# Opening of a two-layer streaming encoder on one core: cached latents on the weights' queue, ScalarE's transfers behind its table load

## The reference

```python
def mla_expand(c_kv, k_rope, w_kvup, qk_k_norm):
    kv = (c_kv @ w_kvup).reshape(B, K, MLA_HEADS, MLA_NOPE_DIM + MLA_V_DIM)
    k_nope, v = kv[..., :MLA_NOPE_DIM], kv[..., MLA_NOPE_DIM:]
    kr = jnp.broadcast_to(k_rope[:, :, None, :], (B, K, MLA_HEADS, MLA_ROPE_DIM))
    k = rmsnorm(jnp.concatenate([k_nope, kr], axis=-1), qk_k_norm)
    return k, v
...
lat_all = jnp.concatenate([past[0], c_kv], axis=1)     # 512 cached latents, then the new ones
kr_all = jnp.concatenate([past[1], k_rope], axis=1)
km, vm = mla_expand(lat_all, kr_all, lp['mla_w_kvup'], lp['mla_qk_k_norm'])
```

## Time and profile before

| | us |
|---|---|
| median of 3 runs | 1043.76 (1043.03 to 1043.83) |
| the profiled execution | 1046.98 |
| span of its instructions | 1045.2 |
| TensorE busy | 1038.1 (99%) |
| VectorE busy | 643.9 (62%) |
| ScalarE busy | 506.6 (48%) |
| GpSimd busy | 314.5 (30%) |

### The profile page before, as it was taken

How to read it: one execution, slowest core, us unless ns; L and a number is a source line. 1 busy time by engine, 2 the same in 40 slices (tenths; PEclk the granted TensorE clock), 3 DMA queues, 4 the chain that set the end, 5 groups by cost and what they waited for, 6 DMA issues and landing times.

```text
span 1045.2 us, 20057 instructions
## 1 busy us (share of the span) xinstructions
PE 1038.1 (99%) x7572; PEld 1003.7 (96%) x7572; DVE 643.9 (62%) x1093; ACT 506.6 (48%) x936; POOL 314.5 (30%) x277
## 2 busy tenths in 40 slices
PE   8999999999999999999999999999999999999998
PEld 6899999999999999999988999999999999999998
DVE  6889764445766666543567996554557565565443
ACT  6567755444554444434354585554445444433341
POOL 2365566531221111100132755656312211111000
PEclk9999999999999999999999999999999999999999
DMA  6465533334535444454513544334344354444541
GB/s 223 114 166 139 186 103 121 92 131 142 161 121 166 156 145 156 142 179 146 176 46 117 167 147 139 94 117 122 122 152 152 122 179 141 155 146 145 158 148 64
DMA packets 49146, 146.27 MB, mean 140 GB/s; under 512 B 8792, under 2 KB 14904, under 8 KB 49080
## 3 DMA queue, kind: packets, MB, share of 16 engines
q1 hardware_dynamic: 42464, 142.86, 43.8%
q10 hardware_dynamic: 6616, 2.50, 1.0%
HBM read 142.11 MB, written 3.22 MB: 139 GB/s over the span
## 4 chain that ended last, share of the span: by engine, by line
PE 98%; DVE 1%; issue 1%; ACT 0%; POOL 0%; ACTq 0%; POOLq 0%
PE psum L585 29%; PE psum L586 29%; PE psum L587 29%; PE psum L786 1%; PE psum L825 1%; PE psum L808 1%; PE psum L816 1%; PE psum L858 1%; PE psum L1047 0%; PE psum L913 0%; PE psum L948 0%; PE psum L687 0%; PE psum L850 0%; PE psum L729 0%; PE psum L722 0%
## 5 line engine op out<-in xcount | busy, mean ns | idle before, releaser
L585 PE MATMUL psum<-AH,WH 128*128 128x320 f32 x1328 | 414.3, 312 | 0.2
L587 PE MATMUL psum<-AH,WL 128*128 128x320 f32 x1328 | 410.3, 309 | 0.0
L586 PE MATMUL psum<-AL,WH 128*128 128x320 f32 x1328 | 410.2, 309 | 0.0
L585 PEld LDWEIGHTS psum<-AH,WH 128*128 128x128 f32 x1328 | 249.2, 188 | 7.4 <-issue 5.5
L586 PEld LDWEIGHTS psum<-AL,WH 128*128 128x128 f32 x1328 | 249.3, 188 | 0.2
L587 PEld LDWEIGHTS psum<-AH,WL 128*128 128x128 f32 x1328 | 249.3, 188 | 0.0
L1130 ACT CAST WH<-raw 128x1024 fp32r<-128x1024 f32 x166 | 172.7, 1045 | 123.2 <-PE psum L587 122.4
L1603 DVE TENSOR_TENSOR WL<-raw,WH 128x1024 fp32r<-128x1024 f32 x103 | 128.9, 1252 | 113.4 <-ACT WH L1130 113.1
L2094 POOL TENSOR_TENSOR WL<-raw,WH 128x1024 fp32r<-128x1024 f32 x60 | 147.7, 2478 | 97.7 <-ACT WH L1130 94.8
L1802 DVE TENSOR_TENSOR WL<-raw,WH 128x1024 fp32r<-128x1024 f32 x88 | 107.5, 1222 | 49.6 <-ACT WH L1313 48.3
L2099 POOL TENSOR_TENSOR fab<-fa,fb 128x320 f32<-128x320 f32 x44 | 38.7, 879 | 264.7 <-DVE fb L1807 264.7
(11 more groups left out here) (296 smaller groups left out, 1580.4 us busy)
## 6 DMA issues: line engine op xcount, KB each, us to landing
raw<-w_all SPq DMA_DIRECT2D x264, 512.0 KB, 3.5
y_out<-X SPq DMA_DIRECT2D x8, 160.0 KB, 2.7
X<-x_in SPq DMA_DIRECT2D x2, 320.0 KB, 5.2
X<-x_in SPq DMA_DIRECT2D x1, 640.0 KB, 7.1
lat_out<-ckv ACTq DMA_DIRECT2D x2, 320.0 KB, 2.9
scratch<-brel SPq DMA_DIRECT2D x8, 63.8 KB, 4.2
bias<-scratch SPq DMA_DIRECT2D x8, 48.0 KB, 3.9
ckv<-lat_in ACTq DMA_DIRECT2D x1, 384.0 KB, 4.5
```

The source lines that it names most:

```text
L585: mm(out, WH[:, slot, c0:c0 + cols], high, start=first, stop=False)
L586: mm(out, WH[:, slot, c0:c0 + cols], low, start=False, stop=False)
L587: return mm(out, WL[:, slot, c0:c0 + cols], high, start=False, stop=last)
```

## The change

The first latents are now issued by SP, ahead of the value weights, and the second latents by ScalarE. On ScalarE the wait for the zeros and the square root (with the table load that stands ahead of it) come first; then the rotary rows are issued and then the second latents. The zero products stay as they are (four rounds).

```diff
     @block.sync
     def _(sp):
         lat = lat_in[0:1].rearrange("a p c n -> (a p) c n")
+        sp.dma_start(ckv[:, :, T:T + 128], lat[:, :, 0:128]).then_inc(s.cache_lat[0], 16)
         sp.dma_start(raw[:, U_KVV, :], w_all[stored(U_KVV)]).then_inc(raw_ready[U_KVV], 16)
         sp.dma_start(raw[:, U_KVK, :], w_all[stored(U_KVK)]).then_inc(raw_ready[U_KVK], 16)
-        sp.dma_start(ckv[:, :, T + 128:T + 256], lat[:, :, 128:256]).then_inc(s.cache_lat[1], 16)
         sp.dma_start(cst[:, K_ID:K_ID + 128], cst_in[:, K_ID:K_ID + 128]).then_inc(s.id_in, 16)
...
-        act.dma_start(ckv[:, :, T:T + 128], lat_in[0:1].rearrange("a p c n -> (a p) c n")[:, :, 0:128]) \
-            .then_inc(s.cache_lat[0], 16)
-        rope_cached(0)
         act.wait_ge(s.warm_zero, 1)
         A(small[:, 31:32], ssum[:, 0:1], ACT.Sqrt)
+        rope_cached(0)
+        act.dma_start(ckv[:, :, T + 128:T + 256], lat_in[0:1].rearrange("a p c n -> (a p) c n")[:, :, 128:256]) \
+            .then_inc(s.cache_lat[1], 16)
         act.wait_ge(raw_ready[U_KVV], 16)
```

## The result

The changed kernel is slower: median 1046.42 us (1044.94 to 1047.0, 14 runs) against 1043.8 us (1042.67 to 1044.21, 14 runs) before, a ratio of 1.0023 (95% interval 1.0015 to 1.0030). I had forecast 1041.0. The profiled execution took 1046.56 us, so it is a usual one of its kernel. The profiled execution of before, at 1046.98, is not: none of the 14 runs came above 1044.21. That turns out to matter most.

What follows compares the result with a forecast made beforehand. TensorE, busy nearly throughout, was taken as the bound, its opening held by the first latents. About 1.2 us (clock) plus 1.5 (hole) gave 2.74 us off the 1043.76 median: 1041.0 us, range 1040.0 to 1043.3.

Steps and rivals of the forecast that it cites:

- The start of that square sets everything later: ScalarE's square of the first key block, at 12.24 us; starting it earlier moves the rest of the program as it stands.
- The opening has no reason to differ by that: Profiled execution stood 3.2 us above the median; the opening's gain of 2.74 us was still taken from the median.
- my own forecast of 9.5: Start of the square of the first keys, forecast at 9.5 us instead of 12.24, 2.74 us earlier.
- my threshold: 0.2% (2.1 us), about what a measurement of this kernel can tell from no change.
- Value weights about 5.0: Opening, SP's queue: value weights land about 5.0 us instead of 4.4, the delay covered by the zero products until 5.91.
- Table load first ... issue ends at 3.9: ScalarE's opening: load and root end at 2.75 us, then the rope rows' issue (1.12 us) ends at 3.9.
- the weighing of load and drain: ScalarE's table load: 1.49 us with root, or ending at 4.12 with a 1.38 us drain; hidden-cost rival 1042.0, chance 0.06.
- my 8.3: Landing of the second latents on ScalarE's queue, issued at 3.9 us; at 8.3 nothing is held.
- the rival "slower": Second latents starve on ScalarE's queue; landing at 12.1 loses 0.8 us, 1044.6; chance 0.07, 0.05 by over 0.2%.
- Key weights 7.35: Opening, SP's queue: key weights land at 7.35 us, unchanged, and become the gate.
- The clock: the rival that I gave 0.07: Clock falls again between 9.45 and 12.86; second block's products at 0.43 us, 1.5 us won, 1042.2; chance 0.07.
- 2.4 GHz from about 6 us on: TensorE's granted clock 1.00 from about 6 us, products 0.23 us apart; about 1.2 us of the gain is the clock.

Runs made afterwards that it cites:

- e2: Kernel before with the two latents' queues swapped, but ScalarE's transfers still issued ahead of the table load; median 1046.41 us, ratio 1.0022.
- e8: The changed kernel, unedited, for a second profile; one time, 1046.18 us.
- e1: The kernel before, unedited, for a second profile; median 1043.09 us, profiled 1042.77, ratio 1.000.
- e9: The kernel before with five rounds of zero products instead of four; median 1044.7 us, ratio 1.0001.
- e10: The changed kernel with ScalarE's two opening transfers moved to SP, plus five rounds of zero products; median 1044.29 us, ratio 1.0000.
- e7: The changed kernel with five rounds of zero products instead of four; median 1045.21 us, ratio 1.0006 to the kernel before.
- e5: The changed kernel with ScalarE's two transfers (rotary rows, second latents) issued on SP behind the key weights; median 1044.29 us, ratio 1.0002 to the kernel before.
- e3: Kernel before, queues unchanged, with only ScalarE's wait for zeros, root and table load ahead of its two transfers; median 1044.88 us, ratio 1.0020.
- e6: The changed kernel with first and second latents in one 256 KB transfer, first on SP; median 1046.36 us, ratio 1.0015 to the kernel before.
- e4: The changed kernel with value weights issued ahead of the first latents on SP; median 1044.96 us, ratio 1.0010 to the kernel before.

## Why the prediction was wrong, step by step

**"The start of that square sets everything later": right.** Time of the execution minus start of the square, over all profiles: before 1034.7, after 1034.8, e2 to e8 1034.7 to 1034.9 throughout; e1, e9 and e10 1034.0 to 1034.1. The last three are 0.7 shorter for a reason below. Nothing was lost behind that square. (SP's later issues did start up to 0.5 us later, against the prediction: the third latents at 5.33 instead of 4.84.)

| profile | value weights landed | first value product | square | its time |
|---|---|---|---|---|
| before | 4.4 | 7.96 | 12.24 | 1046.98 |
| e1, before again | 4.3 | 5.62 | 8.71 | 1042.77 |
| after | 6.0 | 6.82 | 11.72 | 1046.56 |
| e8, after again | 5.9 | 6.67 | 11.39 | 1046.18 |
| e7, after with five rounds | 6.4 | 7.15 | 10.32 | 1045.05 |

**"The opening has no reason to differ by that": the step that failed.** I saw the profiled execution stand 3.2 us above the median and still took a gain worked out in its opening off the median. e1 shows where the 3.2 us lay: in that opening. The 6.3 us landing of the earlier trace rows was that execution's; in e1 and in e9 the same transfer took 4.0, and in e1 the hole and the half-rate products that I meant to remove were not there to remove. Against the 8.71 of e1, even my own forecast of 9.5 is a loss of 0.8. Between executions the landing moved by 2.3 us, more than my threshold. How often before shows the late case is not settled: times above 1046.4 came in 0 of the 14 runs of the result and in 0, 4 and 3 of 33, 29 and 21 runs of before in the later sets. Four of these seven (1046.82 to 1047.26) have a mean granted clock of 0.998, as the profiled execution has with its stretch at 0.50; all other runs of these sets have 1.000. No trace of the seven is on record, so their landings are not known.

**"Value weights about 5.0": mis-sized by 1.0.** I charged the later issue and gave them the 3.6 us of a transfer that goes first. They took 4.5 (e8 4.4, e2 4.3, e7 4.9), landed at 6.0, and so the zero products, which ended at 5.91, did not cover them. Of the 1.65 us by which they are later than before (4.4 to 6.0), 0.75 is the issue behind the first latents, 0.3 what standing second costs without ScalarE's transfers (e5: 3.93 for 3.6), and 0.6 the transfers on ScalarE's queue (4.54 against 3.93). Each is a difference of single executions; by e2, e7, e8 and e10 the last lies between 0.3 and 0.9. The windows from 1.5 to 4.0 and from 3.0 to 4.0 us show the bytes (last two columns: share of the DMA engines, GB/s). First the changed kernel, then e1:

```profile
1.50:4.00 2.50, 2.50 (x5) 1.62 (x6) 0.87 (x5) 0.73 (x2) 1.09 (x2) 1.00 0.50 124
...
3.00:4.00 1.00, 1.00 (x3) 0.68 (x2) 0.59 (x2) 0.00 (x0) 0.00 (x0) 1.00 0.60 145
```

```profile
1.50:4.00 2.50, 2.50 (x5) 1.62 (x6) 0.27 (x3) 1.36 (x2) 1.09 (x2) 1.00 0.86 239
...
3.00:4.00 1.00, 1.00 (x3) 0.67 (x2) 0.00 (x0) 0.99 (x2) 0.00 (x0) 1.00 0.95 360
```

In these 2.5 us the changed kernel moved 310 KB (at 124 GB/s), e1 598 KB. The Trainium skill (DMA: Bandwidth & Descriptors, Issuing engines are not separate DMA queues) has transfers of different engines share the same 16 DMA engines; e5 against the change agrees: with ScalarE's transfers beside them the value weights took 4.54 us, without 3.93. But sharing is not all: between 3 and 4 us the engines are busy 0.60 of the time, so they stand partly idle just when the value weights should run. Without ScalarE's transfers (e5) the same microsecond shows 0.71 and 205 GB/s, still far from e1; with them, but issued from 0.75 on (e2), 0.82 and 252, so it does not go by their presence alone. Nor did ScalarE's transfers hold the value weights where these went first: before, e1 and e3 had them beside and took 3.5 to 3.6. What the DMA engines wait for no run here shows; SP's issue of the value weights itself is longer there, 0.58 us for the 0.40 it takes when it goes first.

**"Table load first ... issue ends at 3.9": wrong.** The queue issues while the load runs (1.25 against 0.75 to 2.03). The 1.38 us drain that the Trainium skill (ScalarE: Activation LUTs, What ACT_TABLE_LOAD costs) adds to a load for every switch to a different set is not seen behind this load: the root starts at 2.04, 0.01 us after the load's end. So the weighing of load and drain was idle. The second latents landed at 8.0, near my 8.3, but by luck: issued at 2.48 and 5.5 us on the way. They held nothing; the kernel is slower, but not by the mechanism of the rival "slower", their late landing.

**"Key weights 7.35": right** (7.45, e8 7.4), but no longer the only gate.

**The clock: the rival that I gave 0.07.** I counted on 2.4 GHz from about 6 us on. The products of both profiles of the changed kernel ran at 0.43 spacing to 10.8 and to about 10.2, after TensorE stood idle 0.91 and 0.77 us. I had priced such a stretch in the second block, not from the first product on. It costs 1.4 to 1.8 us: from the first product to the square it is 4.9 and 4.7 us here, 3.1 to 3.3 in e1, e2, e3, e5 and e7. The times bear this out: with a fifth round (e7) the slow group is gone and the median falls by 1.2.

Among holes this short, the length does not decide: after 0.73 us (e2), 1.00 (e3) and 1.19 (e7) the products ran at the full rate. The profiles differ in when the clock rose. In e1, e6, e7 and e9 it rose during the zero products (eight in 3.88 and 3.99 us, ten in 4.70 and 4.73); in before, e2, e3, e4 and e5 the eight kept to 4.61 to 4.64 us, and the clock had risen by the first value product or shortly after its start. In the two profiles of the changed kernel the eight took 4.64 and 4.63, the hole followed, and the clock rose only 4.0 and 3.6 us into the products. In e10 ten zero products stayed at the lower rate (5.70 us), but no hole followed, and the spacing fell to 0.28 with the second product. That is one trace; with the times of e7 it suggests that a fifth round helps where the clock has not risen by the end of four, and why the rise comes at such different times behind the same work no run here shows. In before and e6 the idle time was 2.05 and 2.10 us; there the clock had risen and fell again, to 0.43 spacing, 1.5 and 0.5 us into the products.

The granted-clock column of the windows stays at 1.00 in the slow stretch of the changed kernel, as it does under the zero products; here the spacing of the products is the better witness.

**Sum.** From e1 to the change the square moves 3.0 us (8.71 to 11.72): 1.2 up to the first product (5.62 to 6.82) and 1.8 between it and the square (3.1 to 4.9), where the products stand at 0.43. These are two single executions; the medians differ by 2.6.

## What to carry to other kernels

Before a gain is worked out from one profile, compare that execution's time with the other runs: if it stands as far off as the gain is large, the gain may be that execution's own accident, and a second profile comes first. In this opening a transfer of 128 KB that went ahead of one of 512 KB delayed it by more than its own issue, and with a second queue busy beside it by more again; bringing one forward has to be charged to every transfer that it passes. And a transfer's landing is read together with what else is in flight, not from a row where it went first.

## What the runs showed of the hardware

The 0.7 us of e1, e9 and e10 is a small surprise. VectorE's product of two 96 x 1 columns (L1843) took 1.24 us in the changed kernel, where it ran beside GpSimd's difference of 128 x 512 and ended with it, and 0.14 us in e1, where that difference began only later. First the changed kernel, then e1:

```profile
15.41 1.24 DVE L1843 TENSOR_TENSOR kgain<-par 96x1 f32<-96x1 f32 x1
...
15.27 1.37 POOL L2157 TENSOR_TENSOR WL<-raw,WH 128x512 fp32r<-128x512 f32 x1 [0.32 <-ACT WH L1130]
```

```profile
12.40 0.14 DVE L1843 TENSOR_TENSOR kgain<-par 96x1 f32<-96x1 f32 x1
...
12.77 1.29 POOL L2157 TENSOR_TENSOR WL<-raw,WH 128x512 fp32r<-128x512 f32 x1 [0.85 <-ACT WH L1130]
```

That VectorE waits for GpSimd there is what the two ends (16.65 and 16.64) suggest. The other profiles fit: in all nine with 1034.7 to 1034.9 this product or the 32 x 1 behind it (L1845) took 1.16 to 1.24 us beside that difference, in e1, e9 and e10 neither took over 0.16. It was not tried by itself. That the table load and the issues of transfers run side by side on ScalarE, and that the same transfer landed after 4.0 or 6.3 us in two executions of one program, I had not expected either.
